# Grouped attention with both heads of a tile in one step

## What is computed

```python
q = _apply_rope(_rmsnorm(aq.reshape(B, L, ATT_HEADS, ATT_HD), q_norm_g), *att_cs)
k = _apply_rope(_rmsnorm(ak.reshape(B, L, ATT_KV_HEADS, ATT_HD), k_norm_g), *att_cs)
v = av.reshape(B, L, ATT_KV_HEADS, ATT_HD)
kc = _rmsnorm(cak.reshape(B, Lc, ATT_KV_HEADS, ATT_HD), k_norm_g)
vc = cav.reshape(B, Lc, ATT_KV_HEADS, ATT_HD)
att = _latent_attention(q.reshape(B, L, ATT_KV_HEADS, ATT_GROUP, ATT_HD), k, v, kc, vc)
# per block of 128 queries:
s = jnp.einsum('bqkgd,bskd->bkgqs', q, k).astype(jnp.float32) * ATT_SCALE
p = jax.nn.softmax(s, axis=-1).astype(v.dtype)
return jnp.einsum('bkgqs,bskd->bqkgd', p, v)
```

## Time and profile before

| | us |
|---|---|
| median of 3 runs | 2010.16 |
| lowest and highest | 2007.03, 2012.57 |
| the profiled execution | 2012.92 |
| its span | 2011.1 |
| start of the attention block's work, its first scores, its last scores, its end | 1430.7, 1454.97, 1573.02, 1584.0 |

### The profile page before, as it was taken

How to read it: one execution, slowest core, us unless ns; L and a number is a source line. 1 busy time by engine, 2 the same in 40 slices (tenths; PEclk the granted TensorE clock), 3 DMA queues, 4 the chain that set the end, 5 groups by cost and what they waited for, 6 DMA issues and landing times. The chain is left out here.

```text
span 2011.1 us, 36554 instructions
## 1 busy us (share of the span) xinstructions
PE 1823.4 (91%) x16014; PEld 1397.2 (69%) x16014; DVE 1011.1 (50%) x1467; ACT 731.7 (36%) x1109; POOL 80.0 (4%) x108
## 2 busy tenths in 40 slices
PE   5999788888978999999999889987599889999997
PEld 3766555765766778888888678853266677888886
DVE  3656445343432656757665753136455445444433
ACT  4355443232312544323223433235434334332322
POOL 0000000000000010001111100000000010000001
PEclk8999898888898999999999999999789999999999
DMA  4211211001004434445563222220000112323231
GB/s 156 74 63 64 102 63 36 34 19 34 30 14 162 141 118 149 149 154 189 199 216 117 66 74 84 84 91 0 12 1 1 53 63 99 101 94 102 91 102 52
DMA packets 49183, 173.47 MB, mean 86 GB/s; under 512 B 5553, under 2 KB 6961, under 8 KB 48129
## 3 DMA queue, kind: packets, MB, share of 16 engines
q1 hardware_dynamic: 39184, 134.62, 19.6%
q0 software_dynamic: 9840, 36.51, 5.4%
HBM read 162.46 MB, written 8.65 MB: 85 GB/s over the span
## 5 line engine op out<-in xcount | busy, mean ns | idle before, releaser
L365 PE MATMUL pair<-h_hi,w_hi 128*128 128x512 f32 x1032 | 418.0, 405 | 36.5 <-DVE w_lo L403 31.4
L367 PE MATMUL pair<-h_hi,w_lo 128*128 128x512 f32 x1032 | 405.5, 393 | 0.0
L366 PE MATMUL pair<-h_lo,w_hi 128*128 128x512 f32 x1032 | 405.4, 393 | 0.0
L403 DVE TENSOR_TENSOR w_lo<-w_raw,w_hi 128x1024 fp32r<-128x1024 f32 (+2 forms) x225 | 265.8, 1183 | 250.2 <-ACT w_hi L388 250.1
L388 ACT CAST w_hi<-w_raw 128x1024 fp32r<-128x1024 f32 (+2 forms) x225 | 221.8, 990 | 202.2 <-PE pair L367 197.4
L365 PEld LDWEIGHTS pair<-h_hi,w_hi 128*128 128x128 f32 x1032 | 196.1, 190 | 96.8 <-DVE w_lo L403 35.9
L366 PEld LDWEIGHTS pair<-h_lo,w_hi 128*128 128x128 f32 x1032 | 196.3, 190 | 42.6 <-issue 4.1
L367 PEld LDWEIGHTS pair<-h_hi,w_lo 128*128 128x128 f32 x1032 | 195.8, 190 | 42.0
L365 PE MATMUL pair<-ff_f_hi,w_hi 128*128 128x512 f32 x512 | 199.7, 390 | 0.5 <-DVE w_lo L403 0.5
L367 PE MATMUL pair<-ff_f_hi,w_lo 128*128 128x512 f32 x512 | 199.2, 389 | 0.0
L366 PE MATMUL pair<-ff_f_lo,w_hi 128*128 128x512 f32 x512 | 199.2, 389 | 0.0
(11 more groups left out here) (430 smaller groups left out, 2688.5 us busy)
## 6 DMA issues: line engine op xcount, KB each, us to landing
w_raw<-in_w_ff SPq DMA_DIRECT2D x128, 512.0 KB, 3.3
mod_w<-in_w_mod POOLq DMA_DIRECT2D x48, 512.0 KB, 3.6
w_raw<-in_w_in SPq DMA_DIRECT2D x22, 512.0 KB, 3.3
w_raw<-in_w_gate SPq DMA_DIRECT2D x16, 512.0 KB, 3.3
w_raw<-in_w_out SPq DMA_DIRECT2D x16, 512.0 KB, 3.3
w_raw<-in_w_rwkv SPq DMA_DIRECT2D x15, 512.0 KB, 3.2
w_raw<-in_w_da SPq DMA_DIRECT2D x12, 512.0 KB, 5.0
g_spill<-norm_pair POOLq DMA_DIRECT2D x16, 256.0 KB, 3.4
```

Source lines behind the costliest of these rows:

```text
L365: nc.tensor.matmul(out, w_hi, x_hi, start=(k == 0), stop=False)
L366: nc.tensor.matmul(out, w_hi, x_lo, start=False, stop=False)
L367: last = nc.tensor.matmul(out, w_lo, x_hi, start=False, stop=(k == kt - 1))
L403: nc.vector.tensor_tensor(lo[:, s % SPLIT_SLOTS, 0:cols], pr.raw[:, w % RAW_SLOTS, 0:cols], hi[:, s % SPLIT_SLOTS, 0:cols].bitcast(F32), A ...
```

## The change

- Loop: 16 steps instead of 32 units. A step is 128 queries of one tile with both its heads g = 0 and 1. Head 0's scores go to PSUM pair 0, head 1's to pair 1, in turn: both heads on the context keys, then both on the others. The scores of step n wait for both exponentials of step n-1.
- PE's order in an iteration is scores of step n, value products of step n-2 (k outer, heads inner, all in bank 7), transposes of step n-1 (head 0, then head 1, over banks 4 to 6).
- The copies of the transposes: ACT two of 512 columns (banks 4 and 6), DVE one of 512 (bank 5). One output bank (7) takes the place of two.
- The items are ordered k, context k, q0 to q3. ACT squares three of them, DVE the other three; the table of Ln is loaded ahead. Tile k and q0 are rotated first, then the scores of step 0 start; the rotations of q1 to q3 follow the scores of step 0 on PE, their sines on DVE come after the maxima of step 0, and their additions one each in steps 0 to 2.
- The products with the cosines are made by GpSimd into a tile of their own.

```diff
-        items = [(A[:, i, :], T) for i in range(5)] + [(B[:, 0, :], TC)]
-        units = [(i, q, g) for i in range(ATT_TILES) for q in range(TB) for g in range(2)]
+        items = [(A[:, 4, :], T), (B[:, 0, :], TC)] + [(A[:, i, :], T) for i in range(4)]
+        turned = [0, 2, 3, 4, 5]
+        steps = [(i, q) for i in range(ATT_TILES) for q in range(TB)]
...
+            @block.gpsimd
+            def _(pool):
+                pool.wait_ge(s["in"], 32)
+                for j, n in enumerate(turned):
+                    pool.wait_ge(s["normed"], n + 1)
+                    nc.gpsimd.tensor_tensor(cos[:, j, :], items[n][0], table[:, 0, :], ALU.mult).then_inc(s["cos"], 1)
...
+                for n in range(N + 2):
+                    if n < N:
+                        i, q = steps[n]
+                        if q == 0:
+                            pe.wait_ge(s["roped"], 2 + i)
+                        if n:
+                            pe.wait_ge(s["exp"], 2 * n)
+                        for cols, key in ((slice(256, 512), B[:, 0, :]), (slice(512, 1024), A[:, 4, :])):
+                            for g in range(2):
+                                h = slice(64 * g, 64 * g + 64)
+                                last = nc.tensor.matmul(pr.pair[g][:, cols], A[h, i, q * P:(q + 1) * P], key[h, :], start=True, stop=True)
+                                if cols.start == 512:
+                                    last.then_inc(s["score"], 1)
                     if n == 0:
+                        pe.wait_ge(s["vout"], 1)
+                        for j in (2, 3, 4):
+                            turn(j)
                     if n >= 2:
                         m = n - 2
+                        i, q = steps[m]
+                        pe.wait_ge(s["tra"], 2 * m + 2)
+                        pe.wait_ge(s["trv"], m + 1)
+                        if q == 0 and i:
+                            pe.wait_ge(s["lo"], i)
                         for k in range(KEY_T):
+                            for g in range(2):
+                                h = slice(64 * g, 64 * g + 64)
+                                last = nc.tensor.matmul(pr.bank[7][h, q * P:(q + 1) * P], vN[:, k, h], probT[:, m % 2, KEYS * g + k * P:KEYS * g + (k + 1) * P],
+                                                        start=(k == 0), stop=(k == KEY_T - 1))
                         last.then_inc(s["pv"], 1)
+                    if 1 <= n <= N:
+                        m = n - 1
+                        for g in range(2):
+                            pe.wait_ge(s["scaled"], 2 * m + g + 1)
...
 # DVE
                 for n, (x, w) in enumerate(items):
                     dve.wait_ge(s["rstd"], n + 1)
...
+                    if n == 2:
+                        rotated(0)
+                        added(0)
+                        rotated(1)
+                        added(1)
+                for n in range(N + 2):
+                    if n < N:
+                        for g in range(2):
...
+                            nc.vector.tensor_reduce(small[:, u % 4, 0:1], pr.pair[g][:, 256:1024], AX_X, ALU.max, negate=True)\
+                                .then_inc(s["negmax"], 1)
+                        if n == 0:
+                            for j in (2, 3, 4):
+                                rotated(j)
+                        for g in range(2):
+                            u = 2 * n + g
+                            dve.wait_ge(s["exp"], u + 1)
...
+                        if n < 3:
+                            added(2 + n)
+                    if 1 <= n <= N:
                         m = n - 1
+                        dve.wait_ge(s["tr"], 2 * m + 2)
...
+                        nc.vector.tensor_copy(probT[:, m % 2, 512:1024], pr.bank[5]).then_inc(s["trv"], 1)
```

More of the change, by code:

```diff
@@ L1769, in _, with turn @@
                 pr.stream(sp, pr.taken + RAW_SLOTS)
+            @block.gpsimd
[4 more added lines that the diff above has]
+                    nc.gpsimd.tensor_tensor(cos[:, j, :], items[n][0], table[:, 0, :], ALU.mult).then_inc(s["cos"], 1)
             @block.tensor
             def _(pe):
+                def turn(j):
+                    n = turned[j]
+                    pe.wait_ge(s["normed"], n + 1)
+                    if j >= 2:
+                        pe.wait_ge(s["sin"], 2)
+                    nc.tensor.matmul(turn_bank(j), rot_sb[:, :], items[n][0], start=True, stop=True).then_inc(s["rot"], 1)
                 for b in range(KEY_T):
@@ L1781, in _ @@
                 pe.wait_ge(s["log"], 6)
-                for n in range(5):
-                    pe.wait_ge(s["normed"], n + 1)
+                pe.wait_ge(s["in"], 32)
+                for j in range(2):
+                    turn(j)
+                pe.wait_ge(s["normed"], 3)
+                for n in range(N + 2):
[11 more added lines that the diff above has]
+                                    last.then_inc(s["score"], 1)
@@ L1784, in _ @@
                     if n == 0:
-                        pe.wait_ge(s["in"], 32)
+                        pe.wait_ge(s["vout"], 1)
+                        for j in (2, 3, 4):
+                            turn(j)
                     if n >= 2:
[L1787 to L1802, removed]
-                        m = n - 2
[L1804 to L1807, removed]
-                        for k in range(KEY_T):
[L1809 to L1821, removed]
-                        last.then_inc(s["pv"], 1)
@@ L1847, in _ @@
                         if m >= 2:
                             act.wait_ge(s["pv"], m - 1)
[L1849 to L1853, removed]
+                        for part in range(2):
+                            act.wait_ge(s["tr"], 2 * m + part + 1)
+                            nc.scalar.copy(probT[:, m % 2, 1024 * part:1024 * part + 512], pr.bank[4 + 2 * part]).then_inc(s["tra"], 1)
@@ L1855, in _, with rotated, added @@
             @block.vector
             def _(dve):
+                def rotated(j):
+                    dve.wait_ge(s["rot"], j + 1)
+                    nc.vector.tensor_tensor(sq[:, turned[j], :], turn_bank(j), table[:, 1, :], ALU.mult).then_inc(s["sin"], 1)
+                def added(j):
+                    x = items[turned[j]][0]
+                    dve.wait_ge(s["sin"], j + 1)
+                    dve.wait_ge(s["cos"], j + 1)
+                    nc.vector.tensor_tensor(x, cos[:, j, :], sq[:, turned[j], :], ALU.add).then_inc(s["roped"], 1)
@@ L1857, in _ @@
+                for n in range(3, 6):
+                    x, w = items[n]
+                    nc.vector.tensor_tensor(sq[:, n, :], x, x, ALU.mult).then_inc(s["sq2"], 1)
                 dve.wait_ge(s["in"], 32)
@@ L1861, in _ @@
                     dve.wait_ge(s["rstd"], n + 1)
[L1862 to L1880, removed]
-                        m = n - 1
[L1882 to L1889, removed]
+                    nc.vector.scalar_tensor_tensor(x, x, qgain[:, :] if n >= 2 else pr.param("k_norm")(0),
+                                                   sq[:, n, 0:w], ALU.mult, ALU.mult).then_inc(s["normed"], 1)
```

74 lines of the change are left out of this document (51 added, 23 removed).

## The result

| | before | after |
|---|---|---|
| median us | 2011.4 (2007.0 to 2012.6, 4 runs) | 1957.3 (1953.8 to 1963.3, 4 runs) |
| the profiled execution | 2012.9 | 1954.7 |
| its span | 2011.1 | 1952.5 |

The ratio is 0.9729, with a 95% interval of 0.9706 to 0.9752: 2.7% faster, 54 us. 1963.5 was forecast, 1954 to 1983 as the range.

A forecast was written before the change was run, and what follows sets the result against it. PE was taken to bound the attention block, all of it exposed. Setup 7.5 us, steps 40.95 and drain -1.8 gave a 46.7 us gain: profiled 2012.9 to 1966.2, median 1963.5, range 1954 to 1983.

The forecast's parts named there:

- Parts 1 and 2: Two heads' scores and value products on PE run side by side: 1.48 us and 1.46 us per step.
- Part 3: Twelve transposes per step on PE take 1.60 us, making PE's step 4.54 us.
- Part 4: Scores wait for both previous exponentials: cycle 4.57 us against PE's 4.54, step taken as 4.6, bounds 4.54 and 5.0.
- Part 5: DVE's and ACT's step work is hidden; extras: 1.2 us in step 0, 0.45 in each of two more, 1.5 for bank 7.
- Part 6: Setup before the first scores: 16.8 us instead of 24.3, with 0.4 for GpSimd collisions.
- The clock's 3 us: Added to the time from first to last scores for a stretch at the lower clock level: 3 us.
- The 1.5 us of collisions in step 0: Behind the first scores: 1.1 us for DVE norming colliding with GpSimd, plus 0.4 for three normings in DVE's queue.
- the clock stayed up behind step 0: Rival, 4%: PE's waits for exponentials drop the clock to 1.2 GHz, step 9.1 us, total 2033.
- The products pack: Rival, 9%, claimed they don't: heads' value products run strictly in turn, PE's step 5.86 us, total 1982.
- the usual step stayed under 5.0: Rival, 15%: a step of 5.0 us from hand-over losses or partly packed products; 7 us less gain, total 1970.
- Nothing packs: Rival, 4%: neither scores nor products run side by side, 7.25 us a step against 7.48, total 2002.

The follow-up runs named there:

- half_max: Kernel after with the maxima over 384 of 768 keys and the queries' gain a tenth: usual step 4.41 us instead of 4.51, block 98.2 instead of 102.8.
- half_transposes: Kernel after without three of each head's six transposes (key blocks 3 to 5): usual step 4.51 us, unchanged; block 102.8, unchanged.
- both_halved: Kernel after with maxima over 384 keys, a tenth of the queries' gain and three of six transposes left out: step 4.08 to 4.20 us, block 97.1.
- pv_by_head: Kernel after with all value products of head 0, then of head 1: median 1970.6 us, 0.9817 of the kernel before; step 5.34 us, block 113.8.
- scores_same_rows: Kernel after with head 0's scores made twice in the same half of the rows, head 1's left out: step 5.70 us instead of 4.51, block 118.6.
- adds_on_gpsimd: Kernel after with the additions of q1 to q3 moved from DVE to GpSimd: block 102.7 us against 102.8, usual step 4.51.
- scores_by_head: Kernel after with head 0's scores on both key parts, then head 1's: step 4.51 us, unchanged; block 103.0 against 102.8.

## Why the prediction was right

- **Bound by PE before; all of it exposed.** Right: what the block lost, 50.5 us, is within the interval of what the kernel lost.
- **Parts 1 and 2, packing.** Right, and shown by taking each away: 1.49 to 1.55 us for both heads' scores and 1.46 for both heads' products, the rows carried over at full size. The Trainium skill's 79% for column tiles (TensorE: Matmul & The Clock Gate, "Measured speedup vs the span model") would have made 1.85 us of the products, an estimate; 24 took 1.53 with their tail where 12 had taken 1.52, so here there is no such loss.
- **Part 3.** 1.46 us (half_max, where PE waits for nothing) instead of 1.60: the twelve transposes follow each other without the second wait. PE's own work is 4.41, not 4.54.
- **Part 4, the cycle.** Right in its terms; 4.51 instead of 4.57, taken as 4.6. That it, not PE's queue, ends last was left open between equals; half_transposes shows it. The path over ACT's first exponential, equally long, was missing, and PE's queue lies 0.1 below the cycle because of part 3.
- **Part 5.** Steps 0 to 3 measured 21.8 us, 0.55 of it the clock's, forecast 22.0 before the clock's term (part 5 puts the 1.2 us of DVE's extra work into step 0, the sum into step 1, where it was measured: 5.68 is 4.51 + 1.17); the steps for bank 7 +0.55 and +0.1, forecast +0.5. With the other steps 0.1 shorter than taken, 73.2 with the clock's part against 74.1 without it.
- **Part 6, setup.** 16.8 as forecast. The collisions with GpSimd came as the row of L2427 said: 1.77 for 0.74.
- **The clock's 3 us** was the mis-sized term: the lower level covered the setup's end and the first 4 us of step 0, and no step behind it in this profile, and cost 0.55 us of the steps. The 1.5 us of collisions in step 0 were 1.2. The steps were forecast 3.9 us too long: 2.45 for the clock and 1.4 for the rest; setup and drain came as forecast, so this is the whole distance from 46.7 to 50.5. That the clock stayed up behind step 0 is in part luck: half_transposes, both_halved and pv_by_head had a stretch at the lower level in step 2, which lasted 6.5 to 7.0 us there. The remaining 3.5 of the 54 us lie outside the block, within what chance does to a total.
- **The rivals.** The products pack; the usual step stayed under 5.0; the clock stayed up behind step 0. "Nothing packs" was not run as a whole, and its parts were priced too high: 1.3 and 1.4 us a step for products and scores, where pv_by_head and scores_same_rows gave back 0.83 and 1.19. One reason is shown: even in pv_by_head some products of the two heads overlap, at the change of heads.
- The Trainium skill (SBUF — State Buffer, "Who interferes with whom") lets DVE's two-port scaling block with GpSimd as well. No row of before showed it. In the kernel after the scalings lasted 0.62, since GpSimd had finished; in adds_on_gpsimd they did collide, 1.29 and 1.43.

## What to carry to other kernels

Matmuls that use half of the array's rows or half of its columns cost their full time each unless their partner in the other half stands close behind them in PE's queue (24 products 1.53 us or 2.43, by the order alone): put the two heads side by side, and look for a place in the old trace where two such groups happen to meet, since that prices the change. When a rewrite takes the cover off a cycle (one buffer per head instead of two in turn), add up the cycle over every engine's path beside the engine's own sum, and stop when they meet. Work moved to GpSimd isn't free where DVE reads two SBUF operands (a norming 1.77 us instead of 0.74) or scales in place (1.29 and 1.43 instead of 0.62) at the same time. And when one early step is late, look at every engine that was late in it: here the slow clock and DVE's stretched normings ended within 0.1 us of each other, and only a run without the first showed that it cost little.

## What was not expected of the hardware

- The next head's instructions start beside the last of this head's: with four in a row for each head nothing was lost (scores, step 4.51), with six 0.27 us of 1.53, with twelve 0.90 (both products). PE even started them ahead of instructions that stand before them in its queue (scores_by_head). The loops needn't alternate strictly.
- GpSimd's addition held up a `tensor_scalar` on DVE that reads one SBUF tile (1.29 and 1.43 us instead of 0.62), which no row of the kernel before shows, and four normings doubled from 2.7 to 5.8 us beside four GpSimd products, while a sine product with one operand in PSUM kept its 0.69.
